# Expert weights in a two-layer trunk: the last of 24 loads issued as five DMAs by partitions

## The reference

```python
N_EXPERTS = 8
TOP_K_EXPERTS = 2
D_FF_EXPERT = 3584

def swiglu(h, w_gate, w_up, w_down):
    return (jax.nn.silu(h @ w_gate) * (h @ w_up)) @ w_down

def moe_ffn(h, router_w, router_b, w_gate, w_up, w_down):
    logits = (h @ router_w).astype(jnp.float32) + router_b.astype(jnp.float32)
    top_v, top_i = lax.top_k(logits, TOP_K_EXPERTS)
    top_p = jax.nn.softmax(top_v, axis=-1)
    gates = jnp.sum(jax.nn.one_hot(top_i, N_EXPERTS, dtype=jnp.float32) * top_p[..., None], axis=-2)
    ...
    for e in range(N_EXPERTS):
        y = y + gates[..., e:e + 1] * swiglu(h, w_gate[e], w_up[e], w_down[e])
    return y
```

## Time and profile before

| what | value |
|---|---|
| median of 3 runs | 1684.12 us (1682.93 to 1684.22) |
| the profiled execution | 1681.39 us, span 1679.6 us |
| PE busy | 1609.5 us, 96% of the span |
| DVE, ACT, POOL busy | 506.3, 221.0, 52.2 us |
| DMA queue 1 (all of the kernel's own transfers) | 459.99 MB, 69.1% of 16 engines' span |
| DMA queue 8 (instructions) | 147 packets, 2.41 MB, 0.5% |
| chain that ended last | PE 86%, DMA 12% |

### The profile page before, as it was taken

The page is one execution under the profiler, slowest core; times in us unless marked ns, Lnnn a source line. Parts: engine busy times, 40 slices in busy tenths (PEclk is TensorE's granted clock), DMA queues, the critical chain, the costliest instruction groups (busy, mean ns, idle before and its releaser), DMA issues.

```text
span 1679.6 us, 40095 instructions
## 1 busy us (share of the span) xinstructions
PE 1609.5 (96%) x18395; PEld 1070.2 (64%) x18395; DVE 506.3 (30%) x960; ACT 221.0 (13%) x463; POOL 52.2 (3%) x126
## 2 busy tenths in 40 slices
PE   8999999999999999999999998999889998899987
PEld 6888878999998888788835443354333543335433
DVE  1456233776633347424221110202002020020201
ACT  2325111100001416111100000000000000000001
POOL 4000200000000000200000000000000000000000
PEclk9999999999999999999999999999999999999999
DMA  9342225443542541223789999999999999999995
GB/s 263 126 151 101 78 78 183 169 166 137 201 149 70 176 144 58 102 91 114 316 315 390 399 426 426 427 426 424 426 426 428 425 425 426 426 428 424 424 428 226
DMA packets 102849, 462.53 MB, mean 275 GB/s; under 512 B 9932, under 2 KB 20862, under 8 KB 78110
## 3 DMA queue, kind: packets, MB, share of 16 engines
q1 hardware_dynamic: 102686, 459.99, 69.1%
HBM read 458.92 MB, written 1.05 MB: 274 GB/s over the span
## 4 chain that ended last, share of the span: by engine, by line
PE 86%; DMA 12%; issue 1%; ACT 0%; DVE 0%; SPq 0%; DVEq 0%
PE bank L1240 24%; PE bank L463 20%; PE bank L1257 11%; DMA slot<-in_moe_w_down 10%; PE bank L1036 8%; PE bank L1121 4%; PE bank L988 3%; PE bank L824 2%; PE bank L944 2%; DMA slot<-in_moe_w_gate 1%; PE bank L1181 1%; PE bank L777 1%; PE bank L1191 1%; PE bank L505 1%; DMA slot<-in_w_in 1%
## 5 line engine op out<-in xcount | busy, mean ns | idle before, releaser
L1240 PE MATMUL bank<-slot,xg 128*32 128x512 f32 (+1 forms) x5120 | 489.8, 540 | 18.3 <-DMA slot<-in_moe_w_up 11.6
L1240 PEld LDWEIGHTS bank<-slot,xg 128*32 128x32 f32 x5120 | 164.4, 110 | 334.3 <-issue 297.8
L463 PE MATMUL bank<-h,slot 128*128 128x256 f32 x1440 | 324.5, 383 | 2.5 <-issue 2.5
L463 PEld LDWEIGHTS bank<-h,slot 128*128 128x128 f32 x1440 | 271.1, 191 | 45.6 <-issue 9.6
L1257 PE MATMUL bank<-slot,aT 128*32 128x256 f32 x4480 | 250.9, 381 | 25.1 <-DMA slot<-in_moe_w_down 23.0
L1257 PEld LDWEIGHTS bank<-slot,aT 128*32 128x32 f32 x4480 | 145.2, 110 | 130.4 <-DMA slot<-in_moe_w_down 28.0
L2648 DVE TENSOR_TENSOR av<-gs,bank 128x512 f32<-128x512 f32 (+1 forms) x40 | 38.1, 952 | 521.5 <-PE bank L1240 521.5
L1924 ACT ACTIVATE gs<-bank 128x512 f32<-128x512 f32 (+1 forms) x40 | 21.8, 544 | 399.7 <-PE bank L1240 399.7
L988 PE MATMUL bank<-sq,slot 128*128 128x256 f32 x256 | 55.9, 379 | 0.0
L1929 ACT ACTIVATE SpT<-bank 128x512 f32<-128x512 f32 x8 | 4.8, 597 | 385.6 <-PE bank L1270 385.6
L988 PEld LDWEIGHTS bank<-sq,slot 128*128 128x128 f32 x256 | 48.5, 190 | 6.5
(11 more groups left out here) (498 smaller groups left out, 1445.4 us busy)
## 6 DMA issues: line engine op xcount, KB each, us to landing
slot<-in_moe_w_gate SPq DMA_DIRECT2D x32, 2048.0 KB, 22.6
slot<-in_moe_w_up SPq DMA_DIRECT2D x32, 2048.0 KB, 27.2
slot<-in_moe_w_down SPq DMA_DIRECT2D x32, 2048.0 KB, 25.4
slot<-in_moe_w_gate SPq DMA_DIRECT2D x32, 1536.0 KB, 25.6
slot<-in_moe_w_up SPq DMA_DIRECT2D x32, 1536.0 KB, 25.2
slot<-in_moe_w_down SPq DMA_DIRECT2D x32, 1536.0 KB, 23.8
slot<-in_w_in SPq DMA_DIRECT2D x18, 2048.0 KB, 7.8
slot<-in_ffn_w_up SPq DMA_DIRECT2D x5, 2048.0 KB, 7.6
```

Of the source, the lines that this page charges most:

```text
L463: ins = mm(o, w[:, k, c:c + n], rhs[:, k, :], start=k == 0, stop=k == nk - 1)
L1240: ins = mm(o.rearrange("s (q x) -> s q x", q=4), xg[:, g, k, :], rows_of(w[:, kk, :], p), start=k == 0, stop=k == KD - 1)
```

## The change

The last load of each expert, n = 23, is issued as five DMAs instead of one: partitions 0 to 95 in one, then 96 to 103, 104 to 111, 112 to 119 and 120 to 127. Each adds 16 to the same semaphore, so the load adds 80. Bytes, sources, destinations and the wait before the load are the same. Slot 2 then sees 16 x 7 = 112 counts for an expert instead of 48, and the waits of PE on that slot count accordingly; those on the other seven slots stay as they were.

```diff
@@ -65,6 +65,7 @@
 NLOAD = 24
+PARTS = ((0, 96), (96, 104), (104, 112), (112, 120), (120, 128))
@@ -1208,7 +1209,12 @@
                 def slot(n):
                     n += NLOAD * s
                     si, r = ring_at(n), n // NSE
-                    pe.wait_ge(slot_full[si], i * 96 + 16 * (loads[si] + r + 1))
+                    if si == ring_at(NLOAD - 1):
+                        per_item = 16 * (NLOAD // NSE - 1 + len(PARTS))
+                        got = (16, 32, per_item)[r % 3] + per_item * s
+                        pe.wait_ge(slot_full[si], i * (2 * per_item) + (16 * loads[si] + got))
+                    else:
+                        pe.wait_ge(slot_full[si], i * 96 + 16 * (loads[si] + r + 1))
                     return slots[si]
@@ -1501,8 +1507,10 @@
+                        src = src.rearrange("o p k n -> (o p) k n")
                         free(n)
-                        sp.dma_start(dst, src.rearrange("o p k n -> (o p) k n")).then_inc(slot_full[ring_at(n)], 16)
+                        for p0, p1 in PARTS if n == NLOAD - 1 else ((0, P),):
+                            sp.dma_start(dst[p0:p1], src[p0:p1]).then_inc(slot_full[ring_at(n)], 16)
                         n += 1
```

## The result

The changed kernel takes 1774.65 us (median of 4 runs, 1769.93 to 1774.91), the kernel before 1684.17 us beside it: a ratio of 1.0528, interval 1.0516 to 1.054. The change makes the kernel 90 us slower, far beyond the 1703 us of the forecast and the 1722 us at which its range ended. The profiled execution has a span of 1772.7 us, 93.1 us more than before.

What follows compares the result with a forecast made beforehand. From about 960 us the sixteen DMA engines' speed in moving expert loads sets the end. SP 0, PE 0 and rows +19 us, added to the 1684.1 us median, gave 1703 us; eight-in-ten range 1677 to 1722 us.

Steps and rivals of the forecast that it cites:

- (1) Who carries the rows: Last loads: eight engines get ten rows, the others six; 6.0 us gained if the early half is burdened, 6.5 lost if late.
- lead of 13.5 us: Expert loads: the early half of the DMA engines runs ahead, covering 13.5 us of the burdened engines' 32 us.
- faster: Rival: partitions don't matter, the early half is burdened and the halves meet at the end; 1678.1 us, chance 0.21.
- (2) Where the rows land: Last loads: narrow DMAs put several engines on few partitions, slowing their writes; +19 us at the end after the lead.
- X: Time of the burdened engines for their four eight-row DMA rows per expert; taken as 5.5 us, possible 1.8 to 16.4 us.
- 2.8 us for the other 96 rows: Burdened engines' time for the 96-row DMA in each last load, added to 5.5 us to make 8.3 us.
- row of w_lora: Two 64-partition loads issued at 16.3 and 17.1 us landed at 179 GB/s, read as at most 3.0 GB/s per partition.
- (3) SP: Issuing four more DMAs costs SP 1.5 us per expert, hidden by its slot waits; zero, 10 us without that cover.
- (4) PE: PE's wait on slot 2 counts seven completions instead of three; below 0.1 us per expert, waiting for the slowest engine as before.
- doubt about the queue's places: SP's load queue: if places count DMAs, five per load leave fewer bytes under way; taken as zero, upper bound 10 us.
- Slower: Whole kernel: outcome of a time above the kernel before, beyond the 0.2% (3.4 us) that can be told; chance 0.65.
- bounds of +9 to +95 us: Change of the end with the early half burdened: four narrow DMAs overlapping entirely, +9 us, or one after another, +95 us.

Runs made afterwards that it cites:

- only96: Against the changed kernel, each expert's last load is only one DMA of partitions 0 to 95, with 96 to 127 left out; 1.0281 of the kernel before, +47 us.
- stride8: Against the changed kernel, the four eight-row DMAs each take every fourth partition of 96 to 127 instead of neighbours; 1.0487 of the kernel before, +82 us.
- stride2: Against the changed kernel, the last load is two DMAs of 64 rows, even partitions and odd partitions; 0.9989 of the kernel before.
- p64_64: Against the changed kernel, the last load is two DMAs of neighbouring partitions, 0 to 63 and 64 to 127; 1.0392 of the kernel before, +66 us.
- extra_cross: Against the changed kernel, last load whole plus eight extra eight-row DMAs (4 KB rows) on every fourth partition of 64 to 127; 1.0157 of the kernel before, +26 us.
- extra_own: Against the changed kernel, last load whole plus eight extra eight-row DMAs (4 KB rows) on every fourth partition of 0 to 63; 1.0067 of the kernel before, +11 us.
- tiny4: Against the changed kernel, the last load is one 128-row DMA again, followed by four eight-partition DMAs of 64 bytes each; 1.0005 of the kernel before.
- extra6: Against the changed kernel, last load whole plus eight extra DMAs of six rows (4 KB each) within partitions 0 to 63; 1.0051 of the kernel before, +9 us.
- extra2: Against the changed kernel, last load whole plus eight extra DMAs of two rows (4 KB each) within partitions 0 to 63; 1.0015 of the kernel before, +2.5 us.

## Why the prediction was wrong

**What bounds the kernel: right.** The DMA engines set the pace of the expert part, and every loss of theirs reached the end.

**(1) Who carries the rows: wrong in both of its cases.** The prediction asked which half the eight engines are, early (three in four) or late. They are six of the one and two of the other. The lead of 13.5 us, which the sum deducted, therefore covered nothing: the end is set by the latest engine, and the two engines in both sets took the full 0.92 us per expert on top of their lag. The end of the changed kernel's DMA work bears this out: a late engine with ten rows falls behind one with six by 4 x 0.46 = 1.8 us per expert, 13 to 15 us over seven or eight, and two engines do work alone for the last 13 us. These 7 us are small beside the rest, but by this reckoning they rule out "faster" even where the partitions cost nothing; no run has the burden without any rows written across. That the upper half fetches the instructions, on which the three in four rested, is shown by no row.

**(2) Where the rows land: right in kind, and the term that was mis-sized.** The forecast put the cost into X, the time of the four narrow DMAs, at 5.5 us, and took the first expert's load as free. Solved backwards, 7 x (2.8 + X - 3.7) - 13.5 = 93 asks for X = 16 us, the end of the range that the text did not believe. But X is the wrong place. The step that failed is the 2.8 us for the other 96 rows: the prediction took them as normal traffic, as though they were dealt like those of a full load. only96 puts that DMA at 5.9 us per expert above the 3.7 us of the whole load, 9.6 us instead of 2.8, some 54 us in all. X itself hardly missed: the changed kernel lies 42 us above only96, 5.2 us per expert for the four narrow DMAs. That near hit is luck. X was worked out from eight neighbouring partitions at 3.0 GB/s each, and stride8 shows that the neighbourhood of the eight rows makes 7 of these 42 us. Put right in the prediction's own sum, 8 x (9.6 + 5.2 - 3.7) with no cover by a lead is 89 us; against the +19 us forecast, 54 us are the 96 rows and 13.5 us the lead that covered nothing.

What the runs show in its place: the cost appears when one DMA's partitions are dealt to the engines in such a way that engines write at the same part of the slot together, on the write side alone, and it hits all sixteen at once (a share of 1.01 at 181 GB/s). The evidence is the pair of stride2 and p64_64 (0 and +66 us with the same DMAs, bytes and rows per engine), the pair with only the partitions or only the memory rows swapped (0 and +75 us), and extra_cross over extra_own (+15 us for the same bytes). That each engine has a part of its own in a DMA of 128 rows is argued from these, not read from a row. The Trainium skill (DMA: Bandwidth & Descriptors, "The descriptor swizzle") states it: in a transfer of 128 partitions each engine writes one port of eight partitions, the lower eight engines in partitions 0 to 63. The runs agree with it, extra_own and extra_cross above all (+11 and +26 us). The Trainium skill (SBUF — State Buffer, "Door 1: The DMA port swizzle") judges a DMA by how many ports its partitions reach. p64_64 and stride2 fit that (eight ports or sixteen), but 96 neighbouring partitions reach all sixteen by the page's map and cost 47 us here, so that count alone doesn't tell a harmless shape; the measurement decides.

**The row of w_lora** was the right one to look at and was read too narrowly. It gave 3.0 GB/s for each partition, and that price was then applied to eight rows, not asked what 64 or 96 rows do. Two DMAs of 64 partitions cost 66 / 8 = 8.3 us per expert here, where two at 179 to 213 GB/s would give 4 to 5 us. The rest is put down to the lag between the halves: each half meets the other's normal traffic at another time. The trace of p64_64 speaks for it. Its windows at the places of the first, second and sixth expert (the last two columns are the DMA share and GB/s):

```profile
900.00:960.00 60.00, 60.00 (x974) 32.82 (x970) 4.85 (x8) 2.84 (x6) 0.00 (x0) 1.00 0.97 371
1020.00:1060.00 40.00, 28.30 (x364) 12.43 (x368) 4.06 (x7) 1.08 (x2) 0.00 (x0) 0.87 1.01 354
1480.00:1520.00 40.00, 27.81 (x320) 12.07 (x316) 4.05 (x7) 1.08 (x2) 0.00 (x0) 0.79 1.01 302
```

Against 391 GB/s before in the first window and 426 in the others, the places lose 3, 7 and 12 us. The half-rate price of 4 to 5 us lies between the first two, and the loss grows while the early half gains its 1.9 us per expert. The first place is no clean case, as the DMA share before is 0.96 there, and no run removes the lag, so it stays likely and not shown.

**(3) SP and (4) PE: right.** tiny4 has the same issues, waits and counts and takes the same time as before (1.0005). The doubt about the queue's places was empty too.

**The chances.** "Slower" had 0.65 and came out, and three of its signs with it: the loads on the chain take 31.69 and 37.91 us, the GB/s row falls at a full share, and PE's waits grow. But the only path to this size was named and dismissed because nothing in the trace is so narrow. An end that has its mechanism and no row against it belongs in the range: with one engine group of unknown place and one unknown price, 1677 to 1722 us was far narrower than the bounds of +9 to +95 us that the text itself had worked out.

## What to carry to other kernels

In a stretch that is bound by the DMA engines, as this one, cut a load so that each piece spans all 128 partitions: by columns (no cost in three pieces), or by every second partition (no cost in two), and not by neighbouring blocks, where two halves cost 66 us and 96 + 32 the same. Before shifting work between DMA engines, find out which engines a narrow DMA uses: add bytes to them alone and look at how many engines stay behind at the end. And a share of 1.0 at half of the usual GB/s was here the sign of engines in each other's way: the share alone doesn't tell it from full speed, so read the GB/s beside it.

## What the runs showed of the hardware that was not expected

A few misplaced rows slow all engines, not only those that carry them: in the 12 us after 1384 us all sixteen are busy and move 181 GB/s together. A DMA of 96 rows, a multiple of 16, costs 5.9 us per expert ((1.0281 - 1) x 1684 / 8) though it moves a quarter less than the load it replaces. And the eight engines of an eight-row DMA are not a half of the sixteen in the sense of who is late: in this kernel, by the ends of extra_own, extra6 and extra2, six of them were early and two late.
